# One 512-column product for both activation halves in the query, key and value projections of a chunked delta-rule layer

## The chip, the cores and the metric

The kernel runs on one core of one Trainium2 chip. The metric is the device time of one execution in microseconds, the median of several runs.

## The reference, cut to what matters

A sequence of 256 tokens with 2048 channels passes a retention layer, a pooling layer and one gated block. The change touches the gated block's delta part: a projection of the normalised activations to query, key and value, a causal convolution of four taps, silu, and the gated delta rule.

```python
qkv = jax.nn.silu(causal_depthwise_conv(qkv, w_conv_qkv[i]))   # SHORT_CONV = 4 taps
q, k, v = jnp.split(qkv, 3, axis=-1)
q, k, v = l2norm(heads(q)), l2norm(heads(k)), heads(v)
o_a = gated_delta_chunked(q, k, v, g_log, beta)                # inverts I + A, lower triangular
o_a = rmsnorm(o_a, g_dn_out[i]).reshape(B, S, DN_WIDTH) * jax.nn.silu(z_a)
```

All is float32. The kernel multiplies in a format of fewer bits, and therefore splits each float32 matrix into a high part and the rest, and adds three products: high x high, high x low, low x high.

## The kernel before, in words

**Weights as a stream.** All weights pass as 900 chunks of 256 x 512 elements through a ring of four buffers. SP loads a chunk (L395), ACT makes the high part (`split_hi`, L626), DVE the rest (`split_lo`, L1078, a subtraction of 1024 elements a partition), PE multiplies. `split_hi` of chunk j + 4 waits until PE has done chunk j. SP may load chunk j + 4 into its buffer once DVE has split chunk j, and SP issues its transfers strictly in the written order. The activations lie transposed, high part `aH` and low part `aL`, each 128 partitions x 16 x 256 tokens.

**Two ways to multiply a chunk.** `chunk_a` (L1917) has the activations as weights and streams the 512 weight columns: 12 products of 512 columns (L1930 to L1932). `chunk_b` (L1946) has 128x128 pieces of the weight as the stationary side and streams the 256 tokens, so that the result is transposed (channels on partitions), as the convolution needs it: for each of 2 values of k and 4 of c three products of 256 columns (L1955, L1957, L1958), which all add into one half of a PSUM bank. PSUM has eight banks of 512 float32 a partition; `half(bank, c)` is half a bank.

**The delta stage** has four blocks (i = 0 to 3; `first` is block 0) of 32 chunks (j = 0 to 31), each for four heads: key in chunks 0 to 7, query in 8 to 15, value in 16 to 23 (`chunk_b`), and the output gate z in 24 to 31 (`chunk_a`). The four take turns on two pairs of banks, 0 and 1, then 2 and 3. Banks 4 to 7 belong to the delta rule. The order of each engine's work is written by hand, against j: after its split for chunk j an engine does what is listed for j, and what is left of the block before (`delta_late`, with n = j + 32; LV is 34). What matters here:

- ACT, j = 7, 15, 23: the first tap (`conv_first`, L857), out of PSUM. DVE, j = 7 to 9, 15 to 17, 23 to 25: the other three taps (`conv`, L1497), 4 instructions each, out of PSUM (in block 0 all three of the key at j = 7, then `decays`, L1411, on which PE's L2201 after chunk 10 waits).
- DVE, j = 13: the matrix A (`aT`, L1574); j = 14: the scaled key (`ke`, L1581) and the scaling of the output of the block before (L1467); j = 18, 19, 20, 22: its transposes (L1092); j = 21: norms and scores; j = 27 to 33: transposes of the value (L1101).
- The inverse: SP at j = 15 sends the 32x32 diagonal pieces of A to memory (L462) and at 16 fetches them back, spread for POOL, which inverts them in 62 small steps (L565, L569, 33 us). At j = 29, behind the load of chunk 37, SP sends the result out (L473) and at 30 fetches it into `iU` (L478). DVE transposes it at n = 32, chunk 0 of the next block (L1429), and PE goes on with it after chunk 2 (n = LV, L2112), the first of a chain of steps for the full inverse and the recurrence.
- After the delta stage a stage of gated chunks follows, at whose start block 3 is finished.

Before the delta stage two chunks of another projection (L2085) go to banks 0 and 1 and 2 and 3, and their result stays in `eE` until POOL has sent it away (L550).

## Time and profile before

| | |
|---|---|
| median of 3 runs | 2625.68 us (2625.46 to 2626.24) |
| span of the profiled execution | 2624.1 us |
| PE busy | 2608.1 us (99%) |
| DVE busy | 1960.0 us (75%) |
| ACT busy | 1321.0 us (50%) |
| POOL busy | 168.0 us (6%) |
| PE's share of the chain that ended last | 97% |
| DMA | 190 GB/s, mean |

The span is that of one profiled execution, 1.6 us below the median of the runs. PE is TensorE, DVE VectorE, ACT ScalarE, POOL GpSimd, SP the engine that issues most transfers. The delta stage lies between 1367 and 1800 us.

### The profile page before, as it was taken

To read this page: it belongs to the slowest core of one execution; us is meant where nothing else is said; L and a number is where in the kernel's file an instruction comes from. 1 tells how busy PE (TensorE), PEld (TensorE's weight loads), DVE (VectorE), ACT (ScalarE), POOL (GpSimd) and SP (SyncE) were. 2 spreads that over 40 slices of the span, in tenths; PEclk is the share of its full clock that TensorE was granted. 3 is DMA by queue.
4 is the path that set the end of the run, shared out by engine and by line. 5 is a ranking of instruction groups with operands and counts; after the bars stand their busy time and mean duration, and the time that the engine had idled before them with its cause. 6 is when DMAs were issued, how large, how long until landed. Compare 5 with 4: busy or idle time off the path is not lost.

```text
span 2624.1 us, 36684 instructions
## 1 busy us (share of the span) xinstructions
PE 2608.1 (99%) x13284; PEld 2218.9 (85%) x13284; DVE 1960.0 (75%) x2764; ACT 1321.0 (50%) x1683; POOL 168.0 (6%) x329
## 2 busy tenths in 40 slices
PE   9999999999999999999999999999999999999998
PEld 7888888888888888888889999998888888788887
DVE  5888877776755766757457786977798999989565
ACT  5444444444444544444456454454666666564453
POOL 0000000000000000000000341413000000000000
PEclk9999999999999999999999999999999999999999
DMA  8555555555655555556655555655555655655754
GB/s 309 179 187 177 179 185 185 184 191 190 198 193 192 195 196 192 196 185 217 196 189 176 173 165 159 194 159 175 176 197 191 197 192 187 200 188 194 247 175 159
DMA packets 151674, 499.69 MB, mean 190 GB/s; under 512 B 28736, under 2 KB 29472, under 8 KB 151008
## 3 DMA queue, kind: packets, MB, share of 16 engines
q1 hardware_dynamic: 148736, 486.18, 56.0%
q0 software_dynamic: 2784, 11.40, 1.4%
q8 instruction: 104, 1.70, 0.3%
q14 instruction: 50, 0.41, 0.0%
HBM read 493.30 MB, written 4.21 MB: 190 GB/s over the span
## 4 chain that ended last, share of the span: by engine, by line
PE 97%; DVE 2%; ACT 1%; issue 0%; DMA 0%; POOL 0%; SPq 0%; DVEq 0%; ACTq 0%
PE PS L1930 27%; PE PS L1932 27%; PE PS L1931 27%; PE PS L1955 4%; PE PS L1957 4%; PE PS L1958 4%; PE PS L2096 2%; DVE yl L1624 1%; DVE wlo L1078 0%; PE PS L2103 0%; PE PS L1966 0%; PE PS L2112 0%; DVE yl L1615 0%; PE PS L2010 0%; PE PS L2020 0%
## 5 line engine op out<-in xcount | busy, mean ns | idle before, releaser
L1078 DVE TENSOR_TENSOR wlo<-raw,whi 128x1024 fp32r<-128x1024 f32 x899 | 1096.9, 1225 | 595.8 <-ACT whi L626 591.1
L626 ACT CAST whi<-raw 128x1024 fp32r<-128x1024 f32 x899 | 939.6, 1049 | 1180.7 <-PE PS L1932 1009.4
L1930 PE MATMUL PS<-whi,aH 128*128 128x512 f32 x2160 | 844.1, 391 | 3.2 <-DVE wlo L1137 1.9
L1931 PE MATMUL PS<-wlo,aH 128*128 128x512 f32 x2160 | 840.6, 389 | 0.0
L1932 PE MATMUL PS<-whi,aL 128*128 128x512 f32 x2160 | 840.6, 389 | 0.0
L1930 PEld LDWEIGHTS PS<-whi,aH 128*128 128x128 f32 x2160 | 405.6, 188 | 88.1 <-issue 2.3
L1932 PEld LDWEIGHTS PS<-whi,aL 128*128 128x128 f32 x2160 | 405.5, 188 | 84.6
L1931 PEld LDWEIGHTS PS<-wlo,aH 128*128 128x128 f32 x2160 | 405.6, 188 | 82.9
L1955 PE MATMUL PS<-aH,whi 128*128 128x256 f32 x768 | 220.8, 288 | 1.5 <-DVE aL L1114 1.5
L1957 PE MATMUL PS<-aL,whi 128*128 128x256 f32 x768 | 217.1, 283 | 0.0
L1958 PE MATMUL PS<-aH,wlo 128*128 128x256 f32 x768 | 217.1, 283 | 0.0
L1932 PE MATMUL PS<-whi,oL 128*128 128x512 f32 x512 | 199.2, 389 | 0.0
L1930 PE MATMUL PS<-whi,oH 128*128 128x512 f32 x512 | 199.2, 389 | 0.0
L1931 PE MATMUL PS<-wlo,oH 128*128 128x512 f32 x512 | 199.2, 389 | 0.0
L1955 PEld LDWEIGHTS PS<-aH,whi 128*128 128x128 f32 x768 | 147.0, 191 | 2.5 <-issue 1.7
L1957 PEld LDWEIGHTS PS<-aL,whi 128*128 128x128 f32 x768 | 147.2, 192 | 0.1
L1958 PEld LDWEIGHTS PS<-aH,wlo 128*128 128x128 f32 x768 | 147.0, 191 | 0.0
L1624 DVE SCALAR_TENSOR_TENSOR yl<-up,wl,yl 128x256 f32<-128x256 f32 x272 | 113.3, 478 | 0.2
L1931 PEld LDWEIGHTS PS<-wlo,oH 128*128 128x128 f32 x512 | 96.1, 188 | 20.1
L1932 PEld LDWEIGHTS PS<-whi,oL 128*128 128x128 f32 x512 | 96.1, 188 | 20.1
L1930 PEld LDWEIGHTS PS<-whi,oH 128*128 128x128 f32 x512 | 96.1, 188 | 19.6
L1930 PE MATMUL PS<-whi,oaH 128*128 128x512 f32 x256 | 99.9, 390 | 0.0
(357 smaller groups left out, 2570.6 us busy)
## 6 DMA issues: line engine op xcount, KB each, us to landing
raw<-in_stream SPq DMA_DIRECT2D x900, 512.0 KB, 3.3
xT<-in_xT SPq DMA_DIRECT2D x4, 512.0 KB, 7.6
H<-in_x SPq DMA_DIRECT2D x4, 512.0 KB, 10.0
pB<-in_pool_b POOLq DMA_DIRECT2D x4, 512.0 KB, 4.5
iT<-diag_in SPq DMA_DIRECT2D x16, 128.0 KB, 3.7
bg<-in_b_gate POOLq DMA_DIRECT2D x8, 256.0 KB, 3.8
out<-eb SPq DMA_DIRECT2D x8, 256.0 KB, 2.2
dmask<-in_dmask SPq DMA_DIRECT2D x4, 384.0 KB, 5.8
```

The costliest lines, as they stand in the source:

```text
L626: nc.scalar.copy(whi[:, s], raw[:, s]).then_inc(hi_done, 1 + blank)
L1078: nc.vector.tensor_tensor(wlo[:, s], raw[:, s], whi[:, s].bitcast(F32), ALU.subtract).then_inc(lo_done, 1 + blank)
L1624: nc.vector.scalar_tensor_tensor(out=to, in0=up[:, c, k:k + SEQ], scalar=w, in1=yl[:, c], op0=ALU.mult, op1=ALU.add).then_inc(long_tap[c], 1)
L1930: mm(out, hi[:, kt + k, tok], whi[:, s, k], start=kt + k == 0, stop=False)
L1931: mm(out, hi[:, kt + k, tok], wlo[:, s, k], start=False, stop=False)
L1932: ins = mm(out, lo[:, kt + k, tok], whi[:, s, k], start=False, stop=last and k == KPC - 1)
L1955: mm(half(bank, c), whi[:, s, k, w], aH[:, kt + k], start=kt + k == 0 and c % 2 == 0, stop=False, skip_group_check=True)
L1957: mm(half(bank, c), whi[:, s, k, w], aL[:, kt + k], start=False, stop=False, skip_group_check=True)
L1958: ins = mm(half(bank, c), wlo[:, s, k, w], aH[:, kt + k], start=False, stop=end, skip_group_check=True)
L2096: ins = mm(PS[rows, bank + n, h * P + at:h * P + at + width], lhsT(t, h), rhs(t, h), start=h == 0, stop=True, skip_group_check=True)
```

## The change

`chunk_b` streams `aH` and `aL` of one k together, as 512 columns out of a joint buffer `aHL`, against the high part of the weight, so that a whole bank holds two partial sums, one for each half; the product of the weight's low part with `aH`, 256 columns, goes to the first half. Each c has a bank of its own, so that a projection has banks 0 to 3, the same ones each time, and z has 4 and 5. The first and last chunks of a projection run column by column. When a column is complete, ACT copies its low half to `xc` in SBUF (`low_half`), DVE adds the other half to it (`both_halves`), and with that the bank is free for the next projection: PE waits on it bank by bank. The taps read `xc`. `xc` takes the place of `eE` in memory. Some of DVE's and ACT's tasks move to other chunks: the scaling of the output from 14 to 16, the scaled key from 14 to 16, the last transposes of the output from 22 to 24, the decays' mask from 6 to 10 and their exponential from 8 to 11 (in blocks 1 to 3), and the splits of chunks 10, 18 and 26 behind the additions. SP's and POOL's orders stay.

```diff
@@ -80,6 +81,7 @@
+EVICT_AT = tuple(b * K16 + K16 - 1 for b in range(3))
@@ -128,8 +130,8 @@
         H = sb(outer, "H", [P, NT, DM])
-        aH = sb(outer, "aH", [P, 16, SEQ], F32R)
-        aL = sb(outer, "aL", [P, 16, SEQ], F32R)
+        aHL = sb(outer, "aHL", [P, 16, 2, SEQ], F32R)
+        aH, aL = aHL[:, :, 0], aHL[:, :, 1]
         cols = sb(outer, "cols", [P, C_END])
@@ -242,7 +244,9 @@
                     pE = sb(b, "pE", [P, NT, SEQ])
-                eE = sb(r, "eE", [P, E_REAL, NT, NB])
+                with ExitStack() as b:
+                    eE = sb(b, "eE", [P, E_REAL, NT, NB])
+                xc = sb(r, "xc", [P, HG, SEQ])
             xn = iT[:].rearrange("p t h n -> p (t h n)")
@@ -316,6 +320,7 @@
+        qkv_ps = sem("qkv_ps")
@@ -781,7 +786,7 @@
                 done(act, q, u)
-                nc.scalar.copy(to, PS[:, 2 * u:2 * u + 2]).then_inc(sem_to, 1)
+                nc.scalar.copy(to, PS[:, 4 * u:4 * u + 2]).then_inc(sem_to, 1)
@@ -850,19 +855,36 @@
+            def low_half(i, y, q, j):
+                n = 3 * i + y
+                if n:
+                    act.wait_ge(conv_tap, n * 16)
+                else:
+                    act.wait_ge(e_out, 16)
+                for c in range(HG):
+                    if c < HG - 1:
+                        act.wait_ge(qkv_ps, n * 3 + c + 1)
+                    else:
+                        done(act, q, j)
+                    nc.scalar.copy(xc[:, c], PS[:, c, SEQ:]).then_inc(conv0_sb, 1)
             def conv_first(i, y):
...
                 for c in range(HG):
+                    act.wait_ge(conv_tap, (3 * i + y) * 16 + c + 1)
                     w = wcv[:, bass.ds(i * (HG * TAPS) + ((1, 0, 2)[y] * 16 * TAPS + c * TAPS + TAPS - 1), 1)]
-                    nc.scalar.activation(yD[:, c], half(2 * (y % 2), c), ACT.Copy, scale=w).then_inc(conv0_sb, 1)
+                    nc.scalar.activation(yD[:, c], xc[:, c], ACT.Copy, scale=w).then_inc(conv0_sb, 1)
...
                         y = 1 if j == 20 else 2
-                        act.wait_ge(conv_tap, i * 36 + 12 * (y + 1))
+                        act.wait_ge(conv_tap, (3 * i + y + 1) * 16)
                         nc.scalar.activation(kqv[:, y], yD[:], ACT.Silu).then_inc(kqv_sb, 1)
+                    if j in EVICT_AT:
+                        low_half(i, EVICT_AT.index(j), q, j)
                     split_hi(q, j + RING)
@@ -881,7 +903,6 @@
                             act.wait_ge(dn_in, 16)
-                        done(act, q, j)
                         conv_first(i, 0)
@@ -891,14 +912,13 @@
                         nc.scalar.activation(ecum[:], cum[:], ACT.Exp).then_inc(cum_sb, 1)
-                    if j == (11 if first else 8):
+                    if j == 11:
                         act.wait_ge(dt_sub, i + 1)
...
                     if j == 10:
-                        act.wait_ge(conv_tap, i * 36 + 12)
+                        act.wait_ge(conv_tap, (3 * i + 1) * 16)
                         nc.scalar.activation(kqv[:, 0], yD[:], ACT.Silu).then_inc(kqv_sb, 1)
                     if j in (15, 23):
-                        done(act, q, j)
                         conv_first(i, j // 8)
@@ -908,7 +928,7 @@
-                nc.scalar.activation(zD[:], PS[:, 2:4], ACT.Silu).then_inc(zd_sb, 1)
+                nc.scalar.activation(zD[:], PS[:, 4:6], ACT.Silu).then_inc(zd_sb, 1)
@@ -1459,7 +1479,7 @@
                                                    op1=ALU.add).then_inc(omean_sb, 1)
-                if n == LV + 12:
+                if n == (LV + 14 if i < D_N - 1 else LV + 12):
                     dve.wait_ge(ors_sb, i + 1)
@@ -1467,8 +1487,8 @@
-                if i < D_N - 1 and n in (LV + 16, LV + 17, LV + 18, LV + 20):
-                    m = (LV + 16, LV + 17, LV + 18, LV + 20).index(n)
+                if i < D_N - 1 and n in (LV + 16, LV + 17, LV + 18, LV + 22):
+                    m = (LV + 16, LV + 17, LV + 18, LV + 22).index(n)
@@ -1487,15 +1507,21 @@
+                n = 3 * i + y
...
-                    src = half(2 * (y % 2), c)
...
-                        dve.wait_ge(conv0_sb, i * 12 + (4 * y + c // 2 * 2 + 2))
+                        dve.wait_ge(conv0_sb, n * 8 + (HG + c // 2 * 2 + 2))
...
-                        dve.wait_ge(conv_tap, i * 36 + (12 * y + HG * (k - 2) + c + 1))
-                    nc.vector.scalar_tensor_tensor(out=yD[:, c, k:], in0=src[:, 0:SEQ - k], scalar=w, in1=yD[:, c, k:],
+                        dve.wait_ge(conv_tap, n * 16 + (HG * (k - 1) + c + 1))
+                    nc.vector.scalar_tensor_tensor(out=yD[:, c, k:], in0=xc[:, c, 0:SEQ - k], scalar=w, in1=yD[:, c, k:],
...
+            def both_halves(i, y):
+                for c in range(HG):
+                    dve.wait_ge(conv0_sb, (3 * i + y) * 8 + c + 1)
+                    nc.vector.tensor_tensor(xc[:, c], PS[:, c, 0:SEQ], xc[:, c], ALU.add).then_inc(conv_tap, 1)
@@ -1528,7 +1554,11 @@
                         log_decays(i, heads(6))
-                    split_lo(q, j + RING)
+                    if j in EVICT_AT:
+                        both_halves(i, EVICT_AT.index(j))
+                        split_lo(q, j - 1 + RING)
+                    if j + 1 not in EVICT_AT:
+                        split_lo(q, j + RING)
                     if first and j in (2, 4):
@@ -1543,21 +1573,16 @@
                         delta_late(i - 1, j + D_PER)
-                    if not first and j == 6:
+                    if first and j == 7:
+                        bias_decays()
+                        for k in range(1, TAPS):
+                            conv(i, 0, k)
+                        decays()
+                    if not first and 7 <= j <= 9:
+                        conv(i, 0, j - 6)
+                    if not first and j == 10:
                         dve.wait_ge(dt_in, i * (16 * NT))
                         log_decays(i, dT)
-                    if j == 7:
-                        if first:
-                            bias_decays()
-                        done(dve, q, j)
-                        if first:
-                            for k in range(1, TAPS):
-                                conv(i, 0, k)
-                            decays()
-                    if not first and 7 <= j <= 9:
-                        conv(i, 0, j - 6)
-                    if j in (15, 23):
-                        done(dve, q, j)
                     if first and j == 14:
@@ -1575,7 +1600,7 @@
                         ins.then_inc(a_sb, 1)
-                    if j == 14:
+                    if j == 16:
                         dve.wait_ge(ke_sb, i * 2 + 1)
@@ -1943,20 +1968,23 @@
-            def chunk_b(q, j, kt, bank, last):
+            def chunk_b(q, j, kt, n, last):
...
-                for k in range(KPC):
-                    for c in range(QT):
-                        w = slice(c * P, (c + 1) * P)
-                        end = last and k == KPC - 1
-                        mm(half(bank, c), whi[:, s, k, w], aH[:, kt + k], start=kt + k == 0 and c % 2 == 0, stop=False,
-                           skip_group_check=True)
-                        mm(half(bank, c), whi[:, s, k, w], aL[:, kt + k], start=False, stop=False, skip_group_check=True)
-                        ins = mm(half(bank, c), wlo[:, s, k, w], aH[:, kt + k], start=False, stop=end,
-                                 skip_group_check=True)
+                by_column = last or kt == 0
+                for a, b in product(range(QT if by_column else KPC), range(KPC if by_column else QT)):
+                    c, k = (a, b) if by_column else (b, a)
+                    if kt + k == 0 and n is not None:
+                        pe.wait_ge(conv_tap, (n - 1) * 16 + c + 1)
+                    w = slice(c * P, (c + 1) * P)
+                    mm(PS[:, c], whi[:, s, k, w], aHL[:, kt + k].rearrange("p a n -> p (a n)"), start=kt + k == 0, stop=False,
+                       skip_group_check=True)
+                    ins = mm(PS[:, c, 0:SEQ], wlo[:, s, k, w], aH[:, kt + k], start=False, stop=last and k == KPC - 1,
+                             skip_group_check=True)
+                    if last and k == KPC - 1 and c < QT - 1:
+                        ins.then_inc(qkv_ps, 1)
@@ -2083,8 +2111,9 @@
             for u in range(E_REAL):
-                pe.wait_ge(h_out, 4 + 5 + u)
-                chunk_a(qe, u, 0, pEh, pEl, 2 * u, True, blank=BLANK if u == E_REAL - 1 else 0)
+                if u == 0:
+                    pe.wait_ge(h_out, 4 + 5)
+                chunk_a(qe, u, 0, pEh, pEl, 4 * u, True, blank=BLANK if u == E_REAL - 1 else 0)
             norm3(0)
@@ -2116,6 +2145,7 @@
                 if n == LV:
+                    pe.wait_ge(zd_sb, i + 1)
                     pe.wait_ge(t0_sb, i + 1)
@@ -2161,23 +2191,21 @@
                     b = j // K16
-                    if j == 0 and not first:
-                        pe.wait_ge(conv_tap, i * 36)
-                    if j == K16 and not first:
-                        pe.wait_ge(zd_sb, i)
-                    if j == 2 * K16 or j == 3 * K16:
-                        pe.wait_ge(conv_tap, i * 36 + 12 * (b - 1))
+                    if j == 3 * K16:
+                        pe.wait_ge(sq_sb, i * 2 + 2)
+                    if first and j == 1:
+                        pe.wait_ge(ee_sb, 2)
                     if first and j in (1, 3, 5):
...
                         pe.wait_ge(ee_sb, 1)
+                        pe.wait_ge(h_out, 4 + 6)
                     if first and b == 0:
...
                     if b < 3:
-                        chunk_b(q, j, (j % K16) * KPC, 2 * (b % 2), j % K16 == K16 - 1)
+                        chunk_b(q, j, (j % K16) * KPC, 3 * i + b if i + b else None, j % K16 == K16 - 1)
                     else:
-                        chunk_a(q, j, (j % K16) * KPC, aH, aL, 2 * (b % 2), j % K16 == K16 - 1)
+                        chunk_a(q, j, (j % K16) * KPC, aH, aL, 4, j % K16 == K16 - 1)
                     delta_late(i, j)
@@ -2242,7 +2270,7 @@
                             if first:
-                                pe.wait_ge(*((zd_sb, D_N) if b else (conv_tap, D_N * 36)))
+                                pe.wait_ge(conv_tap, D_N * 48 - 12)
                         if b == 2:
```

## Rows read from the trace of the kernel before

**Rows 1.** Waits of PE, 1360 to 1870 us: engine line, cause, total us, times, longest us
```profile
PE PS L1955 <- DVE aL L1114: 1.5, 1, 1.5
PE PS L1966 <- DVE XS L1373: 0.5, 1, 0.5
```

**Rows 2.** Timeline of PE, end of chunk 23 in block 1: start us, us, instruction
```profile
1559.64 0.28 PE L1957 MATMUL PS<-aL,whi 128*128 128x256 f32 x1
1559.76 0.28 PE L1958 MATMUL PS<-aH,wlo 128*128 128x256 f32 x1
1559.88 0.40 PE L1930 MATMUL PS<-whi,aH 128*128 128x512 f32 x1
```

**Rows 3.** Timeline of PE, end of block 1, start of block 2
```profile
1581.21 0.39 PE L1931 MATMUL PS<-wlo,aH 128*128 128x512 f32 x1
1581.44 0.39 PE L1932 MATMUL PS<-whi,aL 128*128 128x512 f32 x1
1581.67 0.28 PE L1955 MATMUL PS<-aH,whi 128*128 128x256 f32 x1
```

**Rows 4.** Busy DVE in one window of block 1: length us, busy us
```profile
1529.77:1587.65 57.88, 57.18 (x110) 1.00 0.58 180
```

**Rows 5.** Timeline of DVE, 1529 to 1590 us; groups merged, idle before in brackets
```profile
1529.77 1.22 DVE L1078 TENSOR_TENSOR wlo<-raw,whi 128x1024 fp32r<-128x1024 f32 x1 [2.46 <-ACT whi L626]
...
1533.06 1.22 DVE L1078 TENSOR_TENSOR wlo<-raw,whi 128x1024 fp32r<-128x1024 f32 x1
...
1536.30 1.11 DVE L1581 TENSOR_SCALAR ke<-PS,ed 128x128 f32<-128x128 f32 x4
...
1538.46 1.64 DVE L1497 SCALAR_TENSOR_TENSOR yD<-PS,wcv,yD 128x255 f32<-128x255 f32 x4
...
1571.12 1.86 DVE L1114 SCALAR_TENSOR_TENSOR oaL<-oD_turned,cols,oaH 128x256 fp32r<-128x256 f32 x4
...
1578.58 1.23 DVE L1078 TENSOR_TENSOR wlo<-raw,whi 128x1024 fp32r<-128x1024 f32 x1
...
1586.42 1.23 DVE L1078 TENSOR_TENSOR wlo<-raw,whi 128x1024 fp32r<-128x1024 f32 x1
1588.51 1.25 DVE L1429 STREAM_TRANSPOSE iT<-iU 128x1024 f32<-128x1024 f32 x1 [0.86 <-DMA iU<-diag_out]
```

**Rows 6.** Timeline of DVE and PE at L1429 and L2112, blocks 0, 1, 3
```profile
1479.68 1.25 DVE L1429 STREAM_TRANSPOSE iT<-iU 128x1024 f32<-128x1024 f32 x1 [0.73 <-DMA iU<-diag_out]
...
1482.23 0.43 PE L2112 MATMUL PS<-iT,aT 32*32 32x32 f32 x8
...
1590.39 1.09 PE L2112 MATMUL PS<-iT,aT 32*32 32x32 f32 x32
...
1804.98 1.25 DVE L1429 STREAM_TRANSPOSE iT<-iU 128x1024 f32<-128x1024 f32 x1 [0.75 <-DMA iU<-diag_out]
...
1806.28 0.90 PE L2112 MATMUL PS<-iT,aT 32*32 32x32 f32 x26
```

**Rows 7.** Lines L877 and L1454: duration ns min/median/max, first and last start us
```profile
L877 ACT COPY bT<-PS x1: 374/374/374, 1394.2 to 1394.2; 128x256 f32<-128x256 f32 x1
...
L1454 DVE TENSOR_TENSOR oD<-PS,oD x4: 682/684/685, 1518.7 to 1841.7; 128x512 f32<-128x512 f32 x4
```

**Rows 8.** Timeline of ACT, the first instruction after chunk 15 of block 1
```profile
1534.45 1.05 ACT L626 CAST whi<-raw 128x1024 fp32r<-128x1024 f32 x1 [1.83 <-PE PS L1958]
```

**Rows 9.** Timeline of POOL in block 1, beside two kinds of DVE work
```profile
1569.53 0.30 POOL L565 TENSOR_TENSOR xt<-xi,iT 128x66 f32<-128x66 f32 x1
1569.92 1.46 POOL L569 TENSOR_TENSOR xi<-xi,xt 128x66 f32<-128x66 f32 x1
1571.46 0.36 POOL L565 TENSOR_TENSOR xt<-xi,iT 128x60 f32<-128x60 f32 x1
```

**Rows 10.** Timeline of SP's queue: the inverted diagonal leaves and comes back, block 1
```profile
1581.14 2.55 SPq L473 DMA_DIRECT2D diag_out<-xi  x4
...
1585.06 1.83 SPq L478 DMA_DIRECT2D iU<-diag_out  x4
```

**Rows 11.** Timeline of DVE and PE at the decays of block 0
```profile
1404.76 0.19 DVE L1418 SCALAR_TENSOR_TENSOR gl<-sp,ea 128x32 f32<-128x32 f32 x1
...
1405.95 0.40 PE L2201 MATMUL PS<-gl,con 128*128 128x16 f32 x3
```

**Rows 12.** Two windows at the end: length, busy of PE, PEld, DVE, ACT, POOL, PEclk
```profile
2610.00:2619.00 9.00, 4.87 (x22) 3.70 (x20) 7.59 (x16) 2.30 (x4) 1.11 (x2) 1.00 0.28 102
2619.00:2624.00 5.00, 0.00 (x0) 0.00 (x0) 2.35 (x4) 0.00 (x0) 0.00 (x0) 0.52 0.64 238
```

More of the change, by code:

```diff
@@ L11 @@
 from contextlib import ExitStack
+from itertools import product
 import concourse.bass as bass
```

## The prediction

> **What bounds the kernel now.** I first asked who PE waits for in the delta stage (1360 to 1870 us). In half a millisecond it waits 1.5 us, once, ahead of the first chunk [rows 1]. So PE's own instructions set the time, and the first question is how fast it issues them. The timeline shows starts: two 256-column products follow each other in 0.12 us [rows 2], two 512-column ones in 0.23 us, and a 256-column one follows a 512-column one after 0.23 [rows 3]. The wait behind a product is set by its own width, whatever comes next.
>
> The second question is what runs just short of PE. A window on DVE from 1529.77 to 1587.65, the second half of block 1, has it busy 57.2 of 57.9 us [rows 4], and its timeline has no wait from the split at 1529.77 to the one that ends at 1587.65 [rows 5]. The queue is full, not only busy, for 58 us. It then meets the 32x32 transpose of the inverted diagonal (L1429), for which it waits 0.86 us on a DMA, and PE's first product that reads it (L2112) starts 0.6 us after the transpose ends. In block 3 that product starts 0.06 us after it [rows 6]: PE is held by it already. Blocks 2 and 3 repeat block 1's full queue. Block 0 has no turn of an earlier block's output and some slack. So a chain runs beside PE, from chunk 13 of a block to chunk 2 of the next, with hardly any slack.
>
> **The change, part by part.**
>
> *Two products for three.* A (k, c) step costs 3 x 0.120 = 0.360 us now, and then 0.2267 (2.72 us of a chunk of 12 wide products) + 0.120 = 0.3467. A chunk has 8 steps: 0.107 us less. There are 4 blocks x 3 projections x 8 = 96 such chunks: **10.2 us less** on PE. The joint buffer for the halves costs nothing, its rows keep their length. Column order in first and last chunks, the extra waits when satisfied, and the increments cost nothing visible: every chunk starts with a wait now, and the last product of one and the first of the next are 0.12 apart [rows 2].
>
> *One set of four banks instead of two sets.* The new hand-over is at chunks 7 to 8 and 15 to 16 of each block. In the last chunk a column ends every 0.69 us. ACT copies its low half (0.37 us for 128x256), DVE adds the other (the 512-column add takes 0.68, one of 256 about 0.42) [rows 7]; with 0.1 us per hand-over a bank is free about 1 us after its column. Bank 0 has 2.1 us, and bank 3 is wanted 2.1 us into the next chunk. At chunk 15 DVE is free at 1533.1 [rows 5], column 0 is ready for it at about the same time, and PE wants bank 0 at 1534.0: no stall, with 0.5 us to spare. At chunk 7 both engines are idle enough. I take 0; ends 0 and 1 us at each of 8 places. The third set (chunk 23) has no one waiting for it. Moving z to banks 4 and 5 adds waits on the query's squares and on z's Silu, done 3 us and more ahead of PE: 0.
>
> *Adds on DVE.* Twelve groups of four. At chunk 7 DVE has gaps. At chunk 15 the adds start at 1533.1 and the last needs column 3: ACT hears of the chunk's end at 1534.45 now [rows 8], 0.21 earlier then, copies 0.37, the add ends near 1535.1: **2.0 us** in the full queue. At chunk 23 the queue is late, so the four run in a row, 0.34 each (0.42 less the 0.08 by which neighbours overlap): **1.4 us**. All that is moved on DVE there (output scaling, key scaling, the last turn, splits after adds) stays inside the same full stretch and changes no sum. The masked decays go from chunk 6 to 10, among gaps.
>
> *Taps from SBUF.* The third projection's 12 taps run while POOL inverts. Four taps from PSUM take 1.64; four like operations with both inputs in SBUF take 1.86 beside POOL [rows 5]: 0.055 each, **0.65 us** per block. POOL's operations in that stretch take 0.36 instead of about 0.30, but 1.46 beside a 1024-element subtraction [rows 9].
>
> *What comes late.* In block 1 DVE reaches L1429 at 1587.65 + 2.0 + 1.4 + 0.65 = 1591.7 on the clock of the old trace (chunk 13 held fixed); the product can start at 1591.7 + 1.25 + 0.06 = 1593.0. The DMA path arrives with it: the diagonal is sent out by SP behind a weight load that waits for the split of 1578.58, 4.05 us later then, so it leaves at 1584.6 instead of 1581.14, and 7.4 us from there to the transpose [rows 6, 10] gives 1592.0 at worst. PE would be there at 1590.39 less 13 shortened chunks (14 to 23, 32 to 34) x 0.107 = 1589.0. **Stall 4.0 us**. Block 2 is 0.2 to 0.3 later on DVE, 4.3. Block 3 (10 shortened chunks, since the next are gated ones): DVE's last split ends at 1804.22, plus 4.05, plus 1.31 is 1809.6 against 1806.28 - 1.07 = 1805.2, stall 4.4. In block 0 the DMA path decides: four adds (2.0) stand ahead of the split that the sending waits for, instead of the key scaling and a small one (1.2), and taps beside POOL cost about 0.5, so the transpose starts at 1479.68 + 1.3, the product at 1482.3 against 1482.23 - 1.39: stall 1.4. Also in block 0, two splits and the adds precede the first taps, which delays the decays by more than the 0.8 us which PE gains: they are ready 1.0 us before PE wants them [rows 11]; 0.3 us.
>
> Sum: -10.2 + 4.0 + 4.3 + 4.4 + 1.4 + 0.3 = **+4.2 us**. Each full stretch now lasts longer than PE's share, so the shortened products inside it are lost, and only those in chunks 3 to 13 pay. After the delta stage all starts later by the same amount. The profiled span is 2624.1; the median of the runs is 2625.68, 1.6 more for what lies around it; I add the sum to the median: 2629.9.
>
> **Two rules of the skill.** In the stretch of [rows 9] POOL and two-input operations of DVE slow each other by a few hundredths of a microsecond an operation. The Trainium skill (SBUF — State Buffer, two separate sides) says more: a DVE operation with two SBUF inputs and a GpSimd one exclude each other for the whole instruction. The trace agrees for the subtraction and not for the four small ones. The second is under rival C.
>
> **Rivals.** A: the gain stays. If DVE's queue had slack that I misread, or adds found idle time, only the 10.2 us count, less small things: 2616. For it: the 256/512 rows are firm. Against: no gap in [rows 5], and 0.06 us in block 3 [rows 6]. Half of the delay would give 2622 or so.
>
> B: the taps shut POOL out while they run. Then 12 x 0.39 = 4.7 us join POOL's inverse in every block, in place of 0.5. In block 0, where that path decides, it is +4.2 at once. In the others POOL ends 4.7 later less the 1.0 by which the diagonal leaves earlier, 1584.8, about when SP gets there: +0.2 each. 2634.7. Against it the 0.36 us operations in [rows 9], for it the 1.46. By the page's rule this is what happens.
>
> C: slower by the clock. PE would stand still for 4.0 to 4.4 us three times, and in this trace it was never idle that long between products. At the end it works 4.87 us of the stretch 2610 to 2619 and then stops; the clock granted to 2619 is still 1.00, then 0.52 on average, so it fell some time after the last product [rows 12]. At the lower of the two levels, 1.2 GHz, a chunk takes twice its 2.77 us; one such chunk after three waits is 8 us: 2638. It decides if one of the four waits is long enough for the clock to fall. The Trainium skill (TensorE: Matmul & The Clock Gate, What's actually happening) has the gate fall to half rate after an idle stretch and return after a busy one.
>
> D: the change does not do what it says, the wide product costing more than its columns. The starts in [rows 3] leave no room for it.
>
> **How the numbers follow.** A measurement tells about 0.2% (5.3 us) from no change. The forecast case (full queue decides, 2626 to 2634) gets 0.58, of which 0.18 lies above 2630.9; A whole 0.16; half of A 0.06; B 0.14; C 0.06; D under 0.01. Faster 0.16, same 0.40 + 0.06 = 0.46, slower 0.18 + 0.14 + 0.06 = 0.38. The point is the likeliest case's, 2629.9. The range goes to 2618 (part of A left out) and to 2636 (C left out, B in, and some of the hand-over stalls).
>
> **What would show it.** In the profile after: chunks of 2.77 us; a wait of PE's L2112 for DVE's L1429, four times, 4 us each in blocks 1 to 3 and 1 to 2 us in block 0; DVE with no gap from chunk 13 to L1429, arriving there 4 us later against chunk 13, and next to no wait of L1429 for its DMA; no wait of PE on the adds. If PE does not wait at L2112, the forecast is wrong and the time is A's. If L1429 waits for the DMA for over 1 us, it is B. If the granted clock is below 1.00 around a wait, it is C.

## The result, and the profile after

The changed kernel takes 2639.9 us (median of 5 runs, 2636.3 to 2641.6) against 2625.7 of the kernel before on the same chip: 1.005 of it, with an interval of 1.0038 to 1.0063. It is slower, by more than the forecast said: 14.2 us by the medians where +4.2 stood, and outside the range. The profiled execution has a span of 2639.6 us against 2624.1, 15.5 more, and it is taken apart here.

The waits of PE from 1360 to 1870 us come first (columns as in [rows 1]), then the waits of DVE in the same stretch.

```profile
PE PS L2141 <- issue: 12.0, 3, 5.2
PE PS L1982 <- DVE aHL L1134: 1.6, 1, 1.6
PE PS L1994 <- DVE XS L1393: 0.5, 1, 0.5
```

```profile
DVE iT L1449 <- DMA iU<-diag_out: 3.6, 4, 2.2
```

L2141 is the old L2112, the first product that reads the transposed diagonal; L1449 is the old transpose L1429. PE waited 1.5 and 0.5 before; 12.0 us are new, in three waits in blocks 1 to 3, where the forecast put three of its four. "issue" says that the profile shows no releaser; the timeline of PE (start, us, instruction) at that place in blocks 0 to 3 gives one.

```profile
1482.30 0.87 PE L2141 MATMUL PS<-iT,aT 32*32 32x32 f32 x25
...
1592.51 1.25 PE L2141 MATMUL PS<-iT,aT 32*32 32x32 f32 x32 [3.44 <-issue]
...
1705.96 0.90 PE L2141 MATMUL PS<-iT,aT 32*32 32x32 f32 x14 [5.21 <-issue]
...
1818.83 0.71 PE L2141 MATMUL PS<-iT,aT 32*32 32x32 f32 x10 [3.35 <-issue]
```

The timeline of DVE in block 1, from the end of the scores to that transpose, and the transposes of blocks 2 and 3, as in [rows 5]:

```profile
1532.23 1.26 DVE L1524 TENSOR_TENSOR xc<-PS,xc 128x256 f32<-128x256 f32 x3
1533.76 0.42 DVE L1524 TENSOR_TENSOR xc<-PS,xc 128x256 f32<-128x256 f32 x1 [0.27 <-ACT xc L870]
1534.10 2.35 DVE L1098 TENSOR_TENSOR wlo<-raw,whi 128x1024 fp32r<-128x1024 f32 x2
1536.37 1.67 DVE L1517 SCALAR_TENSOR_TENSOR yD<-xc,wcv,yD 128x255 f32<-128x255 f32 x4
...
1559.89 1.40 DVE L1524 TENSOR_TENSOR xc<-PS,xc 128x256 f32<-128x256 f32 x4
1561.21 2.34 DVE L1098 TENSOR_TENSOR wlo<-raw,whi 128x1024 fp32r<-128x1024 f32 x2
1563.48 1.92 DVE L1517 SCALAR_TENSOR_TENSOR yD<-xc,wcv,yD 128x255 f32<-128x255 f32 x4
...
1568.51 1.86 DVE L1517 SCALAR_TENSOR_TENSOR yD<-xc,wcv,yD 128x254 f32<-128x254 f32 x4
...
1571.53 1.76 DVE L1517 SCALAR_TENSOR_TENSOR yD<-xc,wcv,yD 128x253 f32<-128x253 f32 x4
...
1589.49 1.23 DVE L1098 TENSOR_TENSOR wlo<-raw,whi 128x1024 fp32r<-128x1024 f32 x1
1591.16 1.25 DVE L1449 STREAM_TRANSPOSE iT<-iU 128x1024 f32<-128x1024 f32 x1 [0.45 <-DMA iU<-diag_out]
...
1704.61 1.25 DVE L1449 STREAM_TRANSPOSE iT<-iU 128x1024 f32<-128x1024 f32 x1 [2.22 <-DMA iU<-diag_out]
...
1817.48 1.25 DVE L1449 STREAM_TRANSPOSE iT<-iU 128x1024 f32<-128x1024 f32 x1 [0.16 <-DMA iU<-diag_out]
```

PE's product follows the end of each transpose by 0.1 us: 1591.16 + 1.25 = 1592.41, and it starts at 1592.51. The four adds at chunk 15 take 1532.23 to 1534.10, 1.9 us, those at chunk 23 take 1.3, and from there DVE is full until 1590.71. Between the end of the scores and the transpose lie 58.8 us in block 1, where the kernel before has 55.4 [rows 5, 6].

What the forecast had at 0.06 is in the windows (length, busy time and instructions of PE, PEld, DVE, ACT, POOL, then PE's granted clock, DMA share, GB/s): the first delta chunk; then, for blocks 1 to 3, the wait and what follows it.

```profile
1367.90:1371.30 3.40, 3.11 (x9) 2.67 (x10) 3.40 (x8) 2.65 (x3) 0.66 (x2) 0.50 0.70 226
...
1589.07:1592.51 3.44, 0.01 (x1) 0.04 (x2) 2.96 (x4) 1.04 (x1) 0.00 (x0) 1.00 0.88 220
1593.20:1596.60 3.40, 3.40 (x21) 2.95 (x19) 3.01 (x10) 0.73 (x2) 0.00 (x0) 0.50 0.78 263
1597.00:1606.00 9.00, 9.00 (x91) 7.75 (x90) 3.30 (x4) 3.69 (x4) 0.00 (x0) 1.00 0.59 181
1700.75:1705.96 5.21, 0.00 (x1) 0.03 (x1) 2.96 (x4) 1.18 (x2) 0.00 (x0) 0.99 0.84 230
1705.80:1712.60 6.80, 6.64 (x47) 5.89 (x48) 3.87 (x11) 0.73 (x2) 0.00 (x0) 0.50 0.69 227
1815.47:1818.83 3.36, 0.01 (x2) 0.04 (x2) 3.16 (x5) 1.05 (x1) 0.00 (x0) 0.95 0.72 183
1818.50:1825.30 6.80, 6.47 (x43) 5.39 (x44) 4.03 (x11) 0.73 (x2) 0.00 (x0) 0.50 0.80 230
```

At the end of each wait or just behind it the granted clock falls to 0.50, the lower level (1.2 GHz), for 3.41 or 6.83 us, and is full again after that. In those stretches the wide and the narrow product come at almost twice their distance:

```profile
1588.20 0.40 PE L1982 MATMUL PS<-aHL,whi 128*128 128x512 f32 x1
1588.43 0.28 PE L1984 MATMUL PS<-aHL,wlo 128*128 128x256 f32 x1
1588.55 0.40 PE L1982 MATMUL PS<-aHL,whi 128*128 128x512 f32 x1
...
1594.49 0.63 PE L1982 MATMUL PS<-aHL,whi 128*128 128x512 f32 x1
1594.92 0.41 PE L1984 MATMUL PS<-aHL,wlo 128*128 128x256 f32 x1
1595.13 0.63 PE L1982 MATMUL PS<-aHL,whi 128*128 128x512 f32 x1
```

0.35 us a pair before the wait, 0.64 after it. In the trace the clock is at half for 3.41 + 3.41 + 6.83 + 6.83 = 20.5 us. What that costs PE is read from distances between products, and is less than half of it: 0.8 us of the 20.5 lie inside waits, where nothing is lost, and a pair at the lower level takes 1.84 times as long, not twice. From the product at L2141 to the next group of that line:

```profile
1486.30 0.87 PE L2141 MATMUL PS<-gm,iU 32*32 32x32 f32 x25
...
1597.98 0.69 PE L2141 MATMUL PS<-gm,iU 32*32 32x32 f32 x19
```

That is 4.00 us in block 0, where the clock is full, then 5.47 and 6.91; in block 3, where other chunks lie between, it is 6.81 against 3.94 in e1 below, whose clock stays full. The three falls cost 1.5 + 2.9 + 2.9 = 7.3 us. For the one at the stage's start, the way from the stage's first product to block 0's L2141 takes 114.1 us here and 112.8 in e3 below, which does the same work there with the clock full: 1.3. All four: **8.6 us**.

One loss more is too small for the profile of waits. While z is multiplied in blocks 1 to 3, DVE is so late that PE starts some chunks only when DVE has made their low part: this split in block 1 ends at 1571.61, and the chunk starts 0.05 us later, 0.26 us after the product before it instead of 0.23; the next product is 0.11 late besides.

```profile
1570.30 1.31 DVE L1098 TENSOR_TENSOR wlo<-raw,whi 128x1024 fp32r<-128x1024 f32 x1
...
1571.40 0.39 PE L1957 MATMUL PS<-whi,aHL 128*128 128x512 f32 x1
1571.66 0.50 PE L1955 MATMUL PS<-whi,aHL 128*128 128x512 f32 x1
1572.00 0.39 PE L1956 MATMUL PS<-wlo,aHL 128*128 128x512 f32 x1
```

Four such places a block make 0.5 to 0.6 us. The kernel before has none, and e9 below, whose DVE is less late, has none either.

With this the 15.5 us add up, stretch by stretch. LV0 to LV3 are the starts of the product above in the four blocks; before they are 1482.23, 1590.39, 1698.54 and 1806.28. A shortened chunk counts 0.083 us less (measured below), a wait 0.16 more than its row, because the row counts from a product's end and the next could have started 0.12 after its start.

| stretch | chunks | waits | clock | late splits | later start | sum | measured |
|---|---|---|---|---|---|---|---|
| to LV0 | -2.2 (27) | 0 | +1.3 | 0 | +0.8 | -0.1 | +0.07 |
| LV0 to LV1 | -2.0 (24) | +3.6 | 0 | +0.6 | | +2.2 | +2.05 |
| LV1 to LV2 | -2.0 (24) | +5.4 | +1.5 | +0.5 | | +5.4 | +5.30 |
| LV2 to LV3 | -1.7 (21) | +3.5 | +2.9 | +0.6 | | +5.3 | +5.13 |
| LV3 to the end | 0 | 0 | +2.9 | 0 | | +2.9 | +2.88 |
| all | -8.0 | +12.5 | +8.6 | +1.7 | +0.8 | +15.6 | +15.4 |

The fall behind each LV belongs to the stretch after it. The stage's first product is 0.84 us later (1368.19 against 1367.35), 0.16 of it a longer wait, the rest from stages that the change does not touch; over the kernels run here, but for e10, that start scatters from 1366.9 to 1368.2.

### The profile page after: what moved, and what is told of

The parts are those of the page before. It is cut to its first block, busy times and chain, and to the rows that moved or that the text cites. A ratio compares the mean times of both kernels' runs of the same rounds, so it can differ in the third digit from the quotient of the medians.

```text
span 2639.6 us, 35245 instructions
## 1 busy us (share of the span) xinstructions
PE 2611.4 (99%) x12516; PEld 2182.8 (83%) x12516; DVE 1979.5 (75%) x2812; ACT 1337.9 (51%) x1731; POOL 162.2 (6%) x329
## 4 chain that ended last, share of the span: by engine, by line
PE 96%; DVE 2%; issue 1%; ACT 1%; DMA 0%; POOL 0%; SPq 0%; DVEq 0%; ACTq 0%
PE PS L1955 27%; PE PS L1957 27%; PE PS L1956 27%; PE PS L1982 7%; PE PS L1984 3%; PE PS L2125 2%; DVE yl L1649 1%; DVE wlo L1098 0%; PE PS L2132 0%; PE PS L2141 0%; PE PS L1994 0%; DVE yl L1640 0%; PE PS L2038 0%; DMA raw<-in_stream 0%; PE PS L2047 0%
## 5 line engine op out<-in xcount | busy, mean ns | idle before, releaser
L1955 PE MATMUL PS<-whi,aHL 128*128 128x512 f32 x2160 | 846.2, 392 | 3.3 <-DVE wlo L1157 1.8
L1957 PE MATMUL PS<-whi,aHL 128*128 128x512 f32 x2160 | 841.5, 390 | 0.0
L1956 PE MATMUL PS<-wlo,aHL 128*128 128x512 f32 x2160 | 841.5, 390 | 0.0
L1955 PEld LDWEIGHTS PS<-whi,aHL 128*128 128x128 f32 x2160 | 406.0, 188 | 91.0 <-DVE wlo L1098 4.7
L1957 PEld LDWEIGHTS PS<-whi,aHL 128*128 128x128 f32 x2160 | 406.0, 188 | 85.0
L1956 PEld LDWEIGHTS PS<-wlo,aHL 128*128 128x128 f32 x2160 | 406.2, 188 | 82.9
L1982 PE MATMUL PS<-aHL,whi 128*128 128x512 f32 x768 | 278.6, 405 | 1.6 <-DVE aHL L1134 1.6
L1984 PE MATMUL PS<-aHL,wlo 128*128 128x256 f32 x768 | 216.2, 281 | 0.0
L1982 PEld LDWEIGHTS PS<-aHL,whi 128*128 128x128 f32 x768 | 146.6, 191 | 35.8 <-issue 2.0
L1984 PEld LDWEIGHTS PS<-aHL,wlo 128*128 128x128 f32 x768 | 147.3, 192 | 0.0
L1957 PE MATMUL PS<-whi,oaL 128*128 128x512 f32 x256 | 99.6, 389 | 0.0
L1956 PE MATMUL PS<-wlo,oaH 128*128 128x512 f32 x256 | 99.6, 389 | 0.0
```

The lines of the kernel that those rows point to most:

```text
L1955: mm(out, hi[:, kt + k, tok], whi[:, s, k], start=kt + k == 0, stop=False)
L1956: mm(out, hi[:, kt + k, tok], wlo[:, s, k], start=False, stop=False)
L1957: ins = mm(out, lo[:, kt + k, tok], whi[:, s, k], start=False, stop=last and k == KPC - 1)
L1982: mm(PS[:, c], whi[:, s, k, w], aHL[:, kt + k].rearrange("p a n -> p (a n)"), start=kt + k == 0, stop=False, skip_group_check=True)
L1984: ins = mm(PS[:, c, 0:SEQ], wlo[:, s, k, w], aH[:, kt + k], start=False, stop=last and k == KPC - 1, skip_group_check=True)
```

## The experiments

My theory T after this: the waits come from DVE's full queue, as forecast, and each lets the clock fall, which costs most of the rest. (When I wrote the expectations I took the price as half of the time at the lower level, 10.2 us.) The rivals: the clock's record costs nothing, and something else (wide product, new banks) does; or the DMA path, not DVE's queue, makes the waits (D, where an expectation has that letter; it is not the prediction's rival D). Unless another is named, the edit is to the changed kernel. The kernel before had 2626.65 us beside the first four and 2626.27 beside the next four.

**e1_fill: PE kept busy in the waits.** In blocks 1 to 3, 14 wide products of old data into bank 7, which nobody reads, stand ahead of the wait.

```
                 if n == LV:
+                    pe.wait_ge(qk_sb, i + 1)
+                    for _ in range(14 if i else 0):
+                        mm(PS[:, 7], aH[:, 0, 0:P], aHL[:, 1]..., start=True, stop=True)
                     pe.wait_ge(zd_sb, i + 1)
```

> The changed kernel, with 14 wide products of no use (3.2 us, into a bank that is free there) put ahead of the wait at L2141 in blocks 1 to 3. The main theory (T): the waits of 3.4, 5.2 and 3.4 us come from DVE's late queue, and each then lets the clock fall, for 17 us at half rate in all, which costs some 8.5 us; the filling keeps the clock up and leaves the waits' ends where they are: 2630 to 2633, no stretch at the lower level after LV. The rival (W): the waits alone are the loss, or the wide products run slower for another reason, and the granted clock costs nothing: 2638 to 2642.

Measured: 2630.1 us (2629.0 to 2634.0), ratio 1.0013 (1.0003 to 1.0022). The timeline of PE in block 1, then two windows behind the product in blocks 1 and 2:

```profile
1587.91 3.36 PE L2150 MATMUL PS<-aHL 128*128 128x512 f32 x14
1591.36 1.07 PE L2141 MATMUL PS<-iT,aT 32*32 32x32 f32 x32
```

```profile
1594.00:1603.00 9.00, 9.00 (x90) 7.73 (x89) 4.36 (x5) 3.69 (x4) 0.00 (x0) 1.00 0.71 228
...
1707.00:1716.00 9.00, 9.00 (x74) 7.75 (x73) 3.38 (x5) 3.69 (x4) 0.00 (x0) 1.00 0.61 217
```

Adding 42 products made the kernel almost 10 us faster. In blocks 1 and 3 PE is kept from useful work about as long as before (3.3 us each, 3.4 before), but the clock stays at 1.00 behind it. The 9.8 us are not the clock's alone: in block 2 the transpose waited 2.2 us for its DMA in the changed kernel, which did not recur here, so that PE's stop there is 2.0 us shorter. The other 7.8 are near the 7.3 us by the distances of products. So the time behind the waits is the clock's. The mean granted clock, on record for every execution, says that it was no chance of the profiled ones: 0.994 to 0.996 in the five of the changed kernel, 0.998 or 0.999 in the ten of e1 and in all of the kernel before beside these experiments.

**e2_late: the late half of the triangular solve one chunk later.** Nine steps, LV to LV + 8, move by one chunk on PE, ACT and DVE.

```
+LS = LV + 1
-                if n == LV:
+                if n == LS:
...
-                if n == LV + 8:
+                if n == LS + 8:
```

> The changed kernel, with the nine steps LV to LV + 8 of the late part one chunk later on PE, ACT and DVE (the transpose L1449 and SP's transfers stay where they are). T: PE has 2.8 us more of work before it needs the transpose; the waits shrink to about 0.6, 2.4 and 0.6 us, the clock stays: 2640 less 8.3 less 8.5 = 2621 to 2625. W without a clock effect: 2640 - 8.3 = 2631 to 2633.

Measured: 2625.8 us (2622.9 to 2627.0), ratio 0.9994 (0.9984 to 1.0003). The three waits shrink to 0.85, 1.52 and 0.52 us (2.9 in all, by the profile of waits), and in the profiled execution the clock does not fall. A chunk of 2.8 us took 9.1 of the 12.0 us of waits there, and the falls with them. But that execution is the fastest of ten, 2622.9 us, in the range that I expected; the median is 0.8 above its top. The mean granted clock is 0.999 in the profiled execution and down to 0.997 in others, so in some of them the clock must have been low for 6 us more at least (an estimate: 0.001 of 2622 us is 5.2 us at half clock). One fall of 3.41 us would not be enough; where the others were is not shown.

**e3_defer: 3.5 us a block (1.79 of turns, 1.70 of the split) taken out of DVE's full stretch.** The last four turns of the output and its split move past the transpose, into chunks 4 and 5 of the next block.

```
-                if i < D_N - 1 and n in (LV + 16, LV + 17, LV + 18, LV + 22):
+                if i < D_N - 1 and n in (LV + 16, LV + 17, LV + 18, 2 * D_PER + 4):
...
-                if n == (LV + 24 if i < D_N - 1 else LV + 14):
+                if n == (2 * D_PER + 5 if i < D_N - 1 else LV + 14):
```

> The changed kernel, with the last four transposes of the output (1.8 us) and the split that follows (1.7 us) taken out of DVE's full stretch and done in chunks 4 and 5 of the next block. T: DVE, and SP behind it, reach the transpose L1449 3.5 us sooner: waits of 0, 2 and 0 us, no fall of the clock: 2617 to 2622. The rival (D), that the transfers and the inverse on POOL hold the transpose and not DVE's queue: waits stay, 2636 to 2641.

Measured: 2628.7 us (2627.0 to 2632.1), ratio 1.0008 (0.9998 to 1.0018): a miss for T by 7 us. Waits of 1.83, 2.88 and 1.80 us are left, and the clock falls behind two of them. Timelines in block 1 of POOL's last step of the inverse, of SP's queue, and of DVE at the transpose, which is L1452 here:

```profile
1578.55 0.21 POOL L574 TENSOR_TENSOR xi<-xi,xt 128x8 f32<-128x8 f32 x1
```

```profile
1578.83 2.55 SPq L478 DMA_DIRECT2D diag_out<-xi  x4
...
1583.03 1.83 SPq L483 DMA_DIRECT2D iU<-diag_out  x4
```

```profile
1584.72 1.23 DVE L1101 TENSOR_TENSOR wlo<-raw,whi 128x1024 fp32r<-128x1024 f32 x1
1586.67 1.25 DVE L1452 STREAM_TRANSPOSE iT<-iU 128x1024 f32<-128x1024 f32 x1 [0.72 <-DMA iU<-diag_out]
```

The diagonal leaves 0.07 us after POOL is done, and DVE now waits for it, 2.9 us in blocks 1 to 3: with DVE's queue lighter, POOL and the DMA come next. POOL's inverse also takes longer here, 33.7 to 34.4 us in these blocks against 31.6 to 32.5 in the changed kernel; why is not shown. The rival of the DMA path is right for this part. The rest of the 6.5 us of waits, 3.6, is still DVE's queue: it reaches the transpose 55.9 us after the scores, where the changed kernel has 58.4, which is 2.5 us sooner and not 3.5. A row of ACT and one of DVE in block 1 show where 0.8 of the missing 1.0 went:

```profile
1569.28 1.06 ACT L885 ACTIVATE kqv<-yD 128x1024 f32<-128x1024 f32 x1 [4.01 <-DVE yD L1520]
```

```profile
1571.31 1.23 DVE L1101 TENSOR_TENSOR wlo<-raw,whi 128x1024 fp32r<-128x1024 f32 x1 [0.83 <-ACT whi L631]
```

ACT stands at the value's silu until DVE's last tap is done, and the splits behind the silu on ACT come late for DVE. Blocks 2 and 3 have the same 0.83 and 0.84. Over the ten executions time goes with the granted clock: 2627.0 us at 0.998, 2628.1 to 2629.5 at 0.997, 2630.3 to 2632.1 at 0.996. The number or length of the falls differs between executions of one kernel.

**e4_narrow: three products of 256 columns again**, with all else as changed.

```
-                    mm(PS[:, c], whi[:, s, k, w], aHL[:, kt + k]..., start=kt + k == 0, stop=False, ...)
+                    mm(PS[:, c, 0:SEQ], whi[:, s, k, w], aH[:, kt + k], start=kt + k == 0, stop=False, ...)
+                    mm(PS[:, c, SEQ:], whi[:, s, k, w], aL[:, kt + k], start=False, stop=False, ...)
```

> The changed kernel with the wide product undone: three products of 256 columns, the low half still apart, and the copies, additions, bank waits and moved tasks as in the change. It tells what the change costs without its gain. T: PE comes to each wait 1.4 us later, so waits of about 2.0, 3.8 and 2.0 us; with the clock kept 2633 to 2636, with one fall 2 to 3 more. If the wide products were themselves the cause of the loss (the clock or the pace): 2626 to 2628.

Measured: 2641.2 us (2639.0 to 2645.2), ratio 1.0049 (1.0033 to 1.0066). It misses high, above what I had left for falls of the clock: four waits, the longest of 4.4 us, and the clock at half for 20.5 us in the profiled execution too, which is the slowest of the four. What it tells: with the waits in place the wide product brings 1.3 us by the medians, less than either kernel scatters, and not 8 or 10. While DVE's queue sets the pace, shortening PE mostly lengthens PE's wait.

**e5_both: e2 and e3 together.** No edit of its own.

> The second and the third experiment together: nine steps one chunk later, and four transposes and a split out of DVE's full stretch. T: the transpose starts as in the third experiment, 1.8, 2.9 and 1.8 us too late, and PE needs it 2.8 us later: no wait above 0.3 us, PE bound all along: 2616 to 2618. If a wait of over 1 us is left, something besides DVE's queue and the path over POOL holds PE.

Measured: **2619.1 us** (2617.9 to 2620.5), ratio 0.9972 (0.9961 to 0.9982): faster than both kernels. One wait is left, 1.0 us in block 2, where the transpose waits for its DMA. In the profiled execution, the slowest of the eight (2620.5), the clock falls once, at the 1.6 us ahead of the stage's first chunk. These two, 2.3 to 2.5 us, are about the gap between that execution and the top of what I had expected, 2618.

**e6_sp: the diagonal sent and fetched one weight load earlier on SP's queue.** In the changed kernel it leaves 4.2 us after POOL is done, behind a load that waits for a split of DVE.

```
-                    if j == LV - 5:
+                    if j == LV - 6:
...
-                    if j == LV - 4:
+                    if j == LV - 5:
```

> The changed kernel with SP sending the inverted diagonal one weight load earlier, and fetching it one load earlier. The rival (S): SP's place behind a load that waits for DVE's split is what makes the transpose late (it sends at 51.1 us after the matrix A is done, POOL has finished at 46.9): waits of PE down to 0 to 1 us: 2618 to 2622. T: DVE itself comes to the transpose no sooner, so only its own waits for the transfer go, 0.5, 2.2 and 0.4 us: 2632 to 2637.

Measured: 2636.7 us (2635.9 to 2640.6), ratio 1.0043 (1.0029 to 1.0057). Timeline of DVE in block 1:

```profile
1587.85 1.23 DVE L1098 TENSOR_TENSOR wlo<-raw,whi 128x1024 fp32r<-128x1024 f32 x1
1588.99 1.24 DVE L1449 STREAM_TRANSPOSE iT<-iU 128x1024 f32<-128x1024 f32 x1
```

The transpose has no idle time ahead of it in blocks 1 to 3 and still comes 58.3 us after the scores (58.8, 60.6 and 58.6 in the changed kernel). So DVE's queue alone makes waits of 2.9 to 3.1 us; the DMA path added 0.5, 2.3 and 0.3, nearly all of it in block 2.

**e7_noadd: no adds for the value.** The four adds at chunk 23 go; this kernel leaves out the value's product with the high half of the activations.

```
+                    if y == 2:
+                        dve.sem_inc(conv_tap, 1)
+                        continue
                     nc.vector.tensor_tensor(xc[:, c], PS[:, c, 0:SEQ], xc[:, c], ALU.add).then_inc(conv_tap, 1)
```

> The changed kernel without the four additions of the value projection in each block (the value lacks the sum of the first half; the banks are released as before). T: DVE and SP are 1.4 us sooner at the transpose, the waits of PE fall from 3.4, 5.2, 3.4 to about 2.0, 3.8 and 2.0 us, and there are fewer falls of the clock: 2629 to 2635. If DVE's queue does not matter: 2637 to 2641.

Measured: 2635.2 us (2634.3 to 2638.7), ratio 1.0037 (1.0024 to 1.005). The transpose comes 57.7, 58.3 and 57.4 us after the scores, 1.1 to 1.2 earlier in blocks 1 and 3, as 1.3 us of adds should give. But waits of 2.9 to 3.5 us stay in blocks 1 to 3, one of 0.8 us comes up in block 0, and the clock still falls behind each of the three long ones; I had expected shorter ones, and the time is just past the top of what was forecast. One of several loads taken off the queue is not enough.

**e8_both_narrow: e5 with products of 256 columns**, the edits of e2, e3 and e4.

> The fifth experiment with the wide product undone (three products of 256 columns). With PE bound in both, the difference is what the wide product is worth: T by the starts in the trace 96 chunks x 0.107 = 10.2 us: 2626 to 2628. If the wide product saves less than its starts say, the difference to the fifth is smaller.

Measured: 2626.3 us (2625.9 to 2627.9), ratio 1.0001 (0.9992 to 1.0011), no wait at the transpose and no fall. Four banks, adds, and taps from SBUF cost nothing that shows once they are out of the way of the transpose: LV0 to LV1 takes 108.16 us, as in the kernel before. Against e5 it gives the worth of the wide product by itself: 7.2 us by the medians where 10.2 stood. LV0 to LV1 takes 108.16 us here and 106.16 in e5, 2.0 for 24 chunks or 0.083 a chunk, and 8.0 for 96.

**e9_both_sp and e10_all**, the kernel before at 2626.8 beside them. e9 is e5 with the edit of e6. e10 adds to that twelve products of constants ahead of the stage's first chunk.

```
                     if first and b == 0:
+                        if j == 0:
+                            for _ in range(12):
+                                mm(PS[:, 0, 0:P], con[:, 0], con[:, 1], start=True, stop=True)
                         pe.wait_ge(t_lo, T_N3 * QT + KPC * (j + 1))
```

> Both shifts (nine steps one chunk later, last four turns and their split in the next block) and SP's diagonal copies one weight load earlier. T: what is left of the waits in the kernel with both shifts is one of 1.0 us in block 2, where the late transpose waits for the DMA; SP sends the diagonal a load earlier, so that wait goes: 2617.5 to 2618.7, 0.4 to 1.6 under the 2619.1 of both shifts alone, no wait over 0.3 us in blocks 1 to 3. Rival (POOL's inverse, not SP's place, is what the DMA path ends on): the wait stays at 0.8 to 1.0 and the time at 2619.

> As the run before, and twelve products of constants into bank 0 that nobody reads, put on PE in the 1.6 us in which it waits ahead of the delta stage's first chunk. T: a wait of 1.6 us just there lets the clock fall to half for 3.41 us (1367.2 to 1370.6), which costs 1.7 us; with PE busy it does not fall: 2616 to 2617.3, 1.2 to 1.7 under the run without these products, and a granted clock of 1.00 all through the stage. Rival (the record of the clock there costs nothing, or falls in only some executions): the same time within 0.6 us.

Measured: e9 **2618.2 us** (2617.8 to 2619.6), ratio 0.9967 (0.9955 to 0.9979). Waits of PE, 1360 to 1870 us:

```profile
PE PS L1990 <- DVE aHL L1138: 1.6, 1, 1.6
PE PS L2002 <- DVE XS L1397: 0.5, 1, 0.5
```

The wait in block 2 is gone, as T had it. The time is 0.9 under e5's, but the ranges overlap, and so do the intervals of the ratios: the time alone does not show a gain. e10 took 2619.35 (2619.0 to 2620.2), ratio 0.9972 (0.996 to 0.9983), a miss that tells nothing of the clock: the twelve products (24 in the trace) run 2.6 us instead of the 1.6 that they were to fill and hold the first chunk up (1368.65 against 1367.82), and the clock did not fall there in e9 either. Over ten kernels with that same wait of 1.6 to 1.7 us it fell in four, the changed kernel, e1, e4 and e5. In the windows from 1367.2 to 1370.6, e5 first, then e9:

```profile
1367.20:1370.60 3.40, 3.02 (x9) 2.66 (x10) 3.40 (x8) 2.74 (x3) 0.66 (x2) 0.51 0.71 229
```

```profile
1367.20:1370.60 3.40, 2.78 (x16) 2.48 (x17) 3.40 (x7) 2.98 (x4) 0.66 (x2) 1.00 0.61 189
```

## Why the prediction failed where it did

- **The clock (rival C) was the step that failed.** It had a chance of 0.06 and a price of "one such chunk after three waits is 8 us". It happened behind all three waits, and once at the stage's start: 8.6 us by the distances of products, 7.3 of them behind the three waits, which e1 bears out. The price was about right, though a pair takes 1.84 times as long at the lower level and not twice; the chance was not. The argument against it was only that in the trace of before PE was "never idle that long between products": absence of a case, not a case against. Having forecast three waits of 4 us, I had to carry the clock in the main sum and leave "no fall" as the rival. [Rows 12] showed a fall after PE had stopped, and the rule of the Trainium skill named beside it (TensorE: Matmul & The Clock Gate, What's actually happening) spoke against the change; the trace agrees with it in kind: idle, half rate (0.50), work, full rate (1.00).
- **The full queue was right, and so were its prices.** Adds at chunk 15: 2.0 forecast, 1.9 measured; at chunk 23: 1.4 and 1.3; taps 1.86 for four forecast, 1.92, 1.86 and 1.76 measured.
- **The waits.** 4.0, 4.3 and 4.4 us were forecast in blocks 1 to 3; 3.6, 5.4 and 3.5 came, 12.5 against 12.7. The size agrees, the split does not: in block 2 the DMA path added 2.2, a path that of these three the forecast reckoned for block 1 alone. SP did send the diagonal behind the load that waits for DVE, as forecast, but its fetch in block 2 went out 1.6 us later after the scores than in block 1 (56.7 against 55.0), with the send at 51.1 in both: the four sends held SP's queue for 4.19 us there and for 2.55 in block 1. Why they did is not shown. By the forecast's own sign, "If L1429 waits for the DMA for over 1 us, it is B", this would have been rival B. The sign was a bad one: B is POOL shut out, and POOL's inverse took no longer (below).
- **DVE's lateness at z's chunks** was put at nothing: "PE is held by it" was said of the transpose alone, and the splits that PE needs for z, in the same full queue, were left out. They cost 1.7 us.
- **Block 0** had 1.4 for a stall and 0.3 for the decays. Neither came. The forecast let the transpose start 1.3 us later; it came 54.5 us after the scores, where the kernel before has 54.7. Nor did the later start and the first fall hide a stall: e3, which does the same in block 0 with the clock full and a first product at 1367.26, reaches LV0 at 1480.07 with no wait that shows. It is close there all the same: e7, also with the clock full, waits 0.8 us. Why the adds ahead of the split did not delay the sending was not traced.
- **The shortened products were mis-sized**: -10.2 forecast, -8.0 measured. I had put a wide and a narrow product together from rows of like neighbours, 0.2267 + 0.120 = 0.3467; in alternation they come 0.3485 apart in the mean of 664 pairs of the changed kernel's trace (those at full clock with no pause in them), beside 0.3595 for three narrow ones before, and the stretches between LV0 and LV1 give 0.083 a chunk. The saving is a small difference of two near sums: 0.003 us in 0.35 is a fifth of it.
- **Hand-over of the banks, z's move, SBUF taps: 0**, and e8 shows it. Rival B (taps shut POOL out) fell: POOL's inverse took 31.6 to 32.5 us after and 32.4 to 33.4 before. Taps beside POOL take 0.44 to 0.48 us each, and 0.42 without it. For these small operations the traces disagree with the Trainium skill (SBUF — State Buffer, two separate sides), by which they exclude each other.
- **Rival A** (the gain stays) did not happen, and e8 with e5 shows where its gain was: 8 us, to be had only with the waits gone.

The sum as it should have stood: -8.0 + 12.5 + 8.6 + 1.7 + 0.8 = +15.6, where 15.5 was measured. The 0.8 is for the most part scatter that no forecast could have had.

What stays open: why the clock stays low for 3.41 us after one wait and 6.83 after another of the same length (3.44 and 3.35 in the changed kernel), and why the same 1.6 us ahead of the stage sometimes bring a fall and sometimes not. The size of each fall rests on profiled executions, one a kernel; e1 and the granted clocks of all executions bear out the whole.

## What to carry to other kernels

Ahead of shortening the bound engine, list what runs beside it just short of it, and take its queue off the path first: here the same wide product was worth 8 us with the reader of the transpose 2.8 us later and 3.5 us a block of other work deferred, and the change cost 14 without. Any forecast of waits of some 3 us on TensorE has to carry the clock in its sum; if such a wait can't be removed, products of no use in it can keep the clock: here they gave 7 to 8 us back. When one path is moved away, look up what was to arrive next (here POOL and the DMA, and ACT's splits behind the silu), for that is the new limit.

## What was not expected of the hardware

- The granted clock fell behind each of the 13 waits of 2.7 us and more at that product, over the five kernels that had them (changed, e3, e4, e6, e7), and stood at half for 3.41 or 6.83 us. Behind the nine waits there of 0.3 to 1.8 us it fell once, after 1.80 us in e3, and not after 1.83 us in the same run. These are profiled executions; the granted clocks of the others (e2, e3) show that falls come and go between executions of one kernel.
- A stretch at the lower level cost less than half its length: 2.9 us for 6.83 and 1.5 for 3.41. A wide and a narrow product take 0.64 us there, 1.84 times their distance at full clock.
- A 512-column product and a 256-column one in alternation come 0.002 us further apart than the sum of their distances among their like (0.3485 against 0.3467), which took 1.4 us off the saving over the 768 pairs.
- Taps with both inputs in SBUF take 0.42 us each where POOL stands (1.67 for four, at 1536.37) and 0.44 to 0.48 beside it (1.76 to 1.92); POOL's 32 us of inverse did not get longer beside them in the changed kernel, while it did, to 33.5 us and more, in the kernels with the output's turns moved (e3, e5, e8, e9, e10).
